# Two-layer streaming encoder on one core: another order at the entry of the FFNs and at the first down products, and every sum of weight quarters on GpSimd instead of VectorE

## The reference

```python
def swiglu(x, w_gu, w_dn):
    g, u = jnp.split(x @ w_gu, 2, axis=-1)
    return (jax.nn.silu(g) * u) @ w_dn

h = h + swiglu(rmsnorm(h, norm_ffn[l]), w_gate_up[l], w_down[l])
```

## Time and profile before

| | us |
|---|---|
| three runs | 2456.89, 2457.11, 2457.74 |
| the profiled execution | 2457.27 |
| its span, first to last instruction | 2455.5 |
| TensorE busy in the span | 2409.6 |
| VectorE busy | 1668.2 |
| GpSimd busy | 1002.3 |

### The profile page before, as it was taken

The page is one execution under the profiler, slowest core; times in us unless marked ns, Lnnn a source line. Parts: engine busy times, 40 slices in busy tenths (PEclk is TensorE's granted clock), DMA queues, the critical chain, the costliest instruction groups (busy, mean ns, idle before and its releaser), DMA issues. The chain is left out here.

```text
span 2455.5 us, 42918 instructions
## 1 busy us (share of the span) xinstructions
PE 2409.6 (98%) x16730; PEld 2339.4 (95%) x16730; DVE 1668.2 (68%) x2532; ACT 866.0 (35%) x1765; POOL 1002.3 (41%) x826
## 2 busy tenths in 40 slices
PE   9999999999999999989999999999999999989998
PEld 8989999999999999989999988889999999989997
DVE  7445454439767667688879656757877776778776
ACT  5223232326222222243425556536322222233324
POOL 1222222423544444444447344335544444444542
PEclk9999999999999999999999999999999999999999
DMA  4445566211222222264523233211232332354423
GB/s 161 144 130 147 165 180 187 67 36 38 86 87 98 91 92 99 86 203 143 169 73 73 46 82 99 62 27 35 64 110 72 103 101 91 100 189 147 135 89 123
DMA packets 303533, 259.50 MB, mean 106 GB/s; under 512 B 52856, under 2 KB 261164, under 8 KB 303300
## 3 DMA queue, kind: packets, MB, share of 16 engines
q1 hardware_dynamic: 303140, 256.70, 34.1%
q10 hardware_dynamic: 192, 0.04, 0.0%
HBM read 180.95 MB, written 77.54 MB: 105 GB/s over the span
## 5 line engine op out<-in xcount | busy, mean ns | idle before, releaser
L429 POOL TENSOR_TENSOR wh<-raw,wh 128x512 fp32r<-128x512 f32 x360 | 528.8, 1470 | 610.6 <-ACT wh L423 610.6
L423 ACT ACTIVATE wh<-raw 128x512 fp32r<-128x512 f32 x360 | 227.4, 632 | 706.9 <-PE psum L754 265.4
L754 PE MATMUL psum<-xh,wh 128*128 128x292 f32 (+1 forms) x2560 | 460.5, 296 | 6.4 <-DVE ffn_up L889 4.0
L754 PEld LDWEIGHTS psum<-xh,wh 128*128 128x128 f32 x2560 | 383.5, 189 | 7.2 <-issue 4.2
L754 PE MATMUL psum<-xl,wh 128*128 128x292 f32 (+1 forms) x1280 | 276.6, 298 | 0.0
L2786 PE MATMUL psum<-xh,wh 128*128 128x384 f32 (+1 forms) x792 | 274.6, 347 | 1.3 <-DVE fr_tmp L2976 0.5
L2786 PE MATMUL psum<-xl,wh 128*128 128x384 f32 (+1 forms) x792 | 270.0, 341 | 0.0
L2786 PE MATMUL psum<-xh,wl 128*128 128x384 f32 (+1 forms) x792 | 268.8, 339 | 0.0
L982 DVE TENSOR_TENSOR h<-h,psum 128x584 f32<-128x584 f32 (+1 forms) x280 | 204.9, 752 | 80.6 <-PE psum L779 80.1
L779 PE MATMUL psum<-ffn_slot,wh 128*128 128x292 f32 (+1 forms) x1536 | 206.8, 296 | 0.0
L754 PEld LDWEIGHTS psum<-xl,wh 128*128 128x128 f32 x1280 | 206.4, 189 | 0.0
(11 more groups left out here) (330 smaller groups left out, 5138.1 us busy)
## 6 DMA issues: line engine op xcount, KB each, us to landing
raw<-in_w_gate_up SPq DMA_DIRECT2D x160, 256.0 KB, 3.5
raw<-in_w_down SPq DMA_DIRECT2D x80, 256.0 KB, 3.2
ffn_form_d<-ffn_gate_quarters SPq DMA_DIRECT2D x50, 292.0 KB, 2.2
ffn_form_d<-ffn_gate_quarters SPq DMA_DIRECT2D x50, 288.0 KB, 2.2
raw<-in_a_w_in SPq DMA_DIRECT2D x24, 512.0 KB, 4.8
ffn_slot_raw<-ffn_form_d SPq DMA_DIRECT2D x16, 584.0 KB, 5.2
fr_qkv<-qkv_d SPq DMA_DIRECT2D x36, 256.0 KB, 3.9
ffn_slot_raw<-ffn_form_d SPq DMA_DIRECT2D x16, 576.0 KB, 5.0
```

Of the source, the lines that this page charges most:

```text
L423: act.activation(self.ring(p)[0], self.quarter(b), ACT.Copy).then_inc(self.w_hi, 1)
L429: pool.tensor_tensor(lo, self.quarter(WEIGHT_OF[p % 7]), hi.bitcast(F32), ALU.subtract).then_inc(self.w_lo, 1)
L754: y = pe.matmul(psum[:, bank + c, 0:N], w[:, k, :], x[:, N * c:N * c + N], start=(FRESH[i] and k == 0 and m == 0), stop=(k == 3 and m == 2 ...
```

## The change

1. **The low parts of t1** (four) go from GpSimd, where they stood ahead of the first product of group 0, to VectorE, behind the last entry result; they now count in `x_lo`. The low parts of t3 stand together behind the result of (0, 1), where two stood behind (0, 0) and two behind (0, 1).
2. **The first sum of group 0** waits for 9 finished entry products where it waited for 12; EXTRA and the gate quarters change places in `wl` where that is needed for it.
3. **All weight sums of all groups** are GpSimd's: sum n stands behind the low part of product (g, n).
4. **Hidden forms 1 and 3** of the first chunk on GpSimd: form 1 was made between the low parts for (19, 5) and (19, 6), form 3 behind that for (20, 0). Now form 1 stands behind the low part for (20, 0), and form 3 behind that for (20, 1).

```diff
+        first = 0 in ((1 + base) % 3, (2 + base) % 3)
+        self.extra, _ = at(name + "_w_extra", [P, 512], F32, s["wl_at"] + (0 if first else 3 * 4096 - 2048))
+        self.quad, _ = at(name + "_gate_quarters", [P, 4, T // 2], F32, s["wl_at"] + (2048 if first else 0))
...
-                pool.wait_ge(self.gu_done, self.z["gu_done"] + 12)
+                pool.wait_ge(self.gu_done, self.z["gu_done"] + 9)
...
         self.weight_lo(pool, 3)
-        for k in range(4):
-            self.t1_low(pool, k)
         for g in range(WIDE_GROUPS + DOWN_GROUPS):
             p = 7 * g
             self.product_lo(pool, p)
             if g == WIDE_GROUPS:
+                self.hidden_low(pool, 0, 1, self.t4_lo)
+            self.weight_sum(pool, g, 0)
+            self.product_lo(pool, p + 1)
+            if g == WIDE_GROUPS:
                 self.hidden_low(pool, 0, 3, self.t4_lo)
-            if g == 0:
-                self.weight_sum(pool, g, 0)
-            self.product_lo(pool, p + 1)
-            if g == 0:
-                self.weight_sum(pool, g, 1)
+            self.weight_sum(pool, g, 1)
             self.product_lo(pool, p + 2)
-            if g == 0:
-                self.weight_sum(pool, g, 2)
+            self.weight_sum(pool, g, 2)
             self.product_lo(pool, p + 3)
-            if g == 0:
-                self.weight_sum(pool, g, 3)
+            self.weight_sum(pool, g, 3)
...
             self.product_lo(pool, p + 5)
-            if g == WIDE_GROUPS - 1:
-                self.hidden_low(pool, 0, 1, self.t4_lo)
             self.product_lo(pool, p + 6)
...
         take(self.up, 1, 2, 5, 12)
         product(1, 2, 12)
-        def weight_sums(g, i):
-            if g and i == 1:
-                self.weight_sum(dve, g, 3)
-            if i in (4, 5, 6) and g + 1 < WIDE_GROUPS + DOWN_GROUPS:
-                self.weight_sum(dve, g + 1, i - 4)
+        for k in range(4):
+            t_low(3, k, 24 + k + 1)
...
-                weight_sums(g, i)
...
-                if g == 0 and i < 2:
-                    t_low(4, 2 * i, 32 + 2 * i + 1)
-                    t_low(4, 2 * i + 1, 32 + 2 * i + 2)
+                if g == 0 and i == 1:
+                    for k in range(4):
+                        t_low(4, k, 32 + k + 1)
```

More of the change, by code:

```diff
@@ L171, in __init__ @@
         self.part, _ = at(name + "_part", [P, 2, T // 2], F32, x_end + 6 * pair)
-        self.extra, _ = at(name + "_w_extra", [P, 512], F32, s["wl_at"])
-        self.quad, _ = at(name + "_gate_quarters", [P, 4, T // 2], F32, s["wl_at"] + 2048)
+        first = 0 in ((1 + base) % 3, (2 + base) % 3)
+        self.extra, _ = at(name + "_w_extra", [P, 512], F32, s["wl_at"] + (0 if first else 3 * 4096 - 2048))
+        self.quad, _ = at(name + "_gate_quarters", [P, 4, T // 2], F32, s["wl_at"] + (2048 if first else 0))
         self.late_slots = [(at(name + f"_slot{j}", [P, 2, T], F32R, x_end + n * pair)[0],
@@ L195, in __init__ @@
         self.z = before
-        counts = dict(w_hi=4 + 210 + 2, w_lo=8 + 210 + 4, w_sum=4 * 30, x_hi=40, x_lo=34, x_sq=24, x_sum=21, t_raw=16, t_scaled=8,
-                      t4_lo=8, total=3, root=3, rst=3, gu_done=12 + 140 + 140, gu_evac=12 + 140 + 140, silu=46, hid=46,
+        counts = dict(w_hi=4 + 210 + 2, w_lo=8 + 210 + 4, w_sum=4 * 30, x_hi=40, x_lo=38, x_sq=24, x_sum=21, t_raw=16, t_scaled=8,
+                      t4_lo=4, total=3, root=3, rst=3, gu_done=12 + 140 + 140, gu_evac=12 + 140 + 140, silu=46, hid=46,
                       g_scaled=30, u_scaled=30, hid_hi=41, hid_lo=39, hid_sum=40, dn_done=self.n_down, dn_evac=self.n_down)
@@ L455, in weight_sum @@
         x.then_inc(self.w_sum, 1)
[L457 to L462, removed]
     def t_low_pool(self, pool, k):
@@ L606, in t4_hi @@
             if k < 2:
-                act.wait_ge(self.t4_lo, self.z["t4_lo"] + 4 + k + 1)
+                act.wait_ge(self.t4_lo, self.z["t4_lo"] + k + 1)
             act.activation(self.wide_x(6, k)[0], self.wide_raw(6, k), ACT.Copy).then_inc(self.x_hi, 1)
@@ L742, in wide_product @@
             if g == 0 and i == 3:
-                pe.wait_ge(self.t4_lo, self.z["t4_lo"] + 4)
+                pe.wait_ge(self.x_lo, self.z["x_lo"] + 32)
             if g == 0 and i == 4:
-                pe.wait_ge(self.x_lo, self.z["x_lo"] + 32)
+                pe.wait_ge(self.x_lo, self.z["x_lo"] + 36)
             if g == 0 and i == 6:
-                pe.wait_ge(self.t4_lo, self.z["t4_lo"] + 6)
-                pe.wait_ge(self.x_lo, self.z["x_lo"] + 34)
+                pe.wait_ge(self.t4_lo, self.z["t4_lo"] + 2)
+                pe.wait_ge(self.x_lo, self.z["x_lo"] + 38)
             hi, lo = (w.rearrange("p (k n) -> p k n", k=4) for w in self.ring(p))
@@ L764, in down_product @@
                 if kk == 0 and i in (1, 3):
-                    pe.wait_ge(self.t4_lo, self.z["t4_lo"] + (7 if i == 1 else 8))
+                    pe.wait_ge(self.t4_lo, self.z["t4_lo"] + (3 if i == 1 else 4))
                 elif kk == 0:
```

## The result

The changed kernel takes 2480.53 us, the median of four runs (2479.11 to 2481.74), the kernel before 2457.0 (2456.86 to 2457.74): ratio 1.0094, interval 1.0082 to 1.0106, so 23 us slower. The forecast was slower by 10.8. The profiled execution took 2481.74, its span is 2480.0 against 2455.5, 24.5 more.

The account below looks back on a forecast made before the run. TensorE's own work was taken as the bound (busy 2409.6 of 2455.5 us), changeable only by pauses and the clock behind them. Terms -0.4 + 2.8 + 5.8 + 2.6 = +10.8 gave 2468 us, range 2457 to 2478.

Parts of the forecast that it names:

- Part C: Steady groups: VectorE late at 18 crossings from an up to the next gate group, about 0.3 us each, +5.8.
- Part D: First down products of both FFNs: old pauses and half clock replaced by new waits, +1.3 us each, +2.6.
- Part A: Entry of FFN0: long pause before (0, 1) goes, later products wait for VectorE and GpSimd, about -0.4 us.
- Part B: Entry of FFN1: t1's low parts and two collisions make VectorE late, (0, 4) starts at 1750.2, about +2.8 us.
- The clock holds: Entry of FFN1: no half clock, as no pause was expected to exceed the 1.97 us one that kept full clock.
- the account of busy time against slack: Crossing, four products: the engines' work is 2.4 to 2.5 us too much, VectorE's slack 2.45, leaving 0.05.
- The 0.32: Cost in us per crossing, at 18 crossings, for operations caught by one under way on the other engine; total 5.8.
- the 0.6 before (20, 3): First down products: (20, 3) starts at 1074.0 against 1073.4 us because of sum 2, 0.6 lost.
- its own sign of a higher time: A half clock behind the second down product's pause would show the forecast wrong, with more time; bound another 2.6 us.
- The later down groups: Down groups further on: VectorE makes 2.8 us in 3.22 at most, GpSimd has room enough, no cost.
- The heavier rival: A crossing costs 1.0 us, 2480, or half clock comes at the first down products in both FFNs, 2473; chance 0.11.

Follow-up runs that it names:

- experiment 9: Changed kernel with the first sum of group 0 waiting for 12 finished entry products again, not 9: 2479.80 us.
- experiment 10: Kernel before with hidden forms 1 and 3 of the first chunk made by VectorE instead of GpSimd: 2450.02 us, ratio 0.9970.
- experiments 3 and 4: Changed kernel with VectorE given back the sums of the wide part's gate groups (3: 2466.76 us) or of its up groups (4: 2481.80 us).
- Experiments 5 and 6: Changed kernel with one GpSimd operation added at each crossing (5: 2468.52 us), or with sum 2 directly behind sum 1 in groups 1 to 19 (6: 2467.66 us).
- Experiments 2 and 12: Kernel before with all sums on GpSimd (2: 2475.34 us); the same plus hidden forms 1 and 3 on VectorE and sum 2 behind sum 1 (12: 2461.88 us).

## Why the prediction was wrong

The direction was right and so were most of the places; the size was not: 10.8 forecast, 24.5 in the profiled execution. Of the 13.7 between them, 5.9 are Part C, 3.2 the clock at the entries, 2.1 Part D and 2.4 that execution's start and end.

- **Part A**: -0.4 forecast for the start of (0, 4), -0.4 measured, with the pauses before (0, 1) to (0, 3) at 0.46, 1.55, 0.94 as described.
- **Part B**: +2.8 forecast, +2.7 measured. Its reason was half right: the low parts of t1, not the earlier sum, for which Part B counted two collisions and which gains 1.0 in experiment 9.
- **The clock, the step that failed first.** Part B says: "The clock holds, as no pause exceeds the 1.97 that was harmless", and Part A looks for a long pause before (0, 1) alone. The working's own numbers say otherwise. In Part A (0, 3) at 613.6 and 3.22 of work end at 616.8, and (0, 4) starts at 620.2, a pause of 3.4; Part B's times, spaced alike, imply one of 3.7. Measured 3.33 and 3.28, each with half clock behind it: 3.2 us. A term for it belonged in A and B, as the trace before shows the like behind 3.97. Nor was 1.97 a safe bound: in experiment 10 the same pause of 1.97 was followed by 0.50,

```profile
1745.90:1749.20 3.30, 3.30 (x16) 3.30 (x15) 2.40 (x2) 1.20 (x2) 3.30 (x3) 0.50 0.02 6
```

- **Part C**, the term that was mis-sized: 5.8 forecast, 11.7 measured (5.4 and 6.3). The place was right (experiments 3 and 4) and so was the waiting resource, VectorE's result. The step that failed is the account of busy time against slack, with an average of half a collision on top. Experiments 5 and 6 show that the balance of busy time does not give the price: with more work on the same path the two wide stretches cost 1.1 us in all over the kernel before, with the same work in another order 2.8, in the changed kernel 12.1 by the same measure, (0, 5) to (19, 0). The 0.32 was the 0.05 that the account left plus half of the 0.54 by which one operation outlasted another; that one such half would do was a guess. In the crossing's rows every one of the three `form_sum` operations stands behind one of GpSimd. The price was to be had only by laying both engines' operations side by side through one crossing, in time, with the restart of TensorE that each short pause costs.
- **Part D**: +2.6 forecast, +4.7 measured (2.9 and 1.9), and by other shares. In FFN0 the pauses behind GpSimd were 1.3 as forecast and 4.07 where 3.4 was; the 0.6 before (20, 3) was not there. In FFN1 the first wait is for VectorE already, at (20, 0), and the one behind GpSimd 2.50. TensorE's waits for VectorE were 2.4 in FFN0 and 3.9 in FFN1, and not 5. What filled the sum is half clock in two windows each, 3.1 and 3.4, which the working had as a bound and not as a term (its own sign of a higher time, half clock behind the second down product's pause, came), and 1.0 and 0.8 by slower products beside the pauses.
- **The later down groups** were forecast as nothing ("room enough"), and cost nothing. The last 2.4 belong to that execution's start and end, and are partly the distance of 2481.74 from the median.

The heavier rival was nearest in time (2480 for 1.0 at a crossing, or 2473 for half clocks at the first down products). What happened is a part of each: 0.6 to 0.7 a crossing, and half clocks at the entries as well as at the first down products. It had a chance of 0.11; the range ended at 2478.

By the rule of the Trainium skill's GPSIMD Engine Reference, § 4.1 Engine selection, elementwise work with two inputs belongs on VectorE. Experiments 2 and 12 agree for this kernel: 18 and 12 us for the same sums on GpSimd. Its § 1 Specifications, row on SBUF interfaces, says that GpSimd shares them with VectorE and that VectorE instructions with two SBUF inputs contend; the rows of the crossing agree, with 1.85 for a `form_sum` against 0.76.

## What to carry to other kernels

Where two engines share a path, moving work from one to the other does not empty the first: ask which operations will run side by side, and put what needs the path beside what does not (here, a copy out of PSUM). A balance of busy time finds the place where it will hurt, not the price; an experiment that adds work and comes out faster says that the phase, which operation runs beside which, decides. Write down each pause that your own forecast implies, and price the clock behind it.

## What the runs showed that was not expected

Eighteen GpSimd operations more made the kernel 12 us faster (2468.52 against 2480.53). A 512-wide sum on VectorE took 3.13 us beside a 1168-wide subtraction on GpSimd, against 0.68 alone. A pause of TensorE of 0.14 in the profile cost 0.37 in the pace of products (0.29 before the row of 665.39, 0.08 in it). Pauses of 1.9 to 2.0 us were followed by half clock in some executions (1.93 and 1.99 after, 1.97 in experiment 10) and not in others (1.97 before, 1.95 in experiment 3); of those over 3 us none was without it.
